# A hybrid attention layer on one core: first loads on two queues, first operations in another order

## What is computed

```python
h = rms_norm(x, norm_pre_g[layer])
proj = jnp.einsum('bsd,de->bse', h, w_in[layer])
q_a, k_a, v_a, g_a, f_a, q_b, k_b, v_b, g_b = jnp.split(proj, offsets, axis=-1)
log_f = jax.nn.log_sigmoid((f_a + fox_forget_b[layer]).astype(jnp.float32))
y_a = fox_attention(..., log_f)     # 8 heads of 64, causal, with F = cumsum(log_f) added to the logits
y_a = merge_heads(y_a) * jax.nn.silu(g_a)
y_b = moba_attention(..., slopes)   # 8 heads of 64, causal with ALiBi (a single block here)
y_b = merge_heads(y_b) * jax.nn.silu(g_b)
y = jnp.einsum('bse,ed->bsd', jnp.concatenate([y_a, y_b], axis=-1), w_out[layer])
x = x + rms_norm(y, norm_post_g[layer])
```

## Time and profile before

| | us |
|---|---|
| median of 3 executions | 163.12 |
| lowest and highest | 162.9 and 168.15 |
| span of the profiled execution | 161.2 |
| DVE busy | 124.8 (77%) |
| ACT busy | 112.3 (70%) |
| POOL busy | 72.0 (45%) |
| bytes moved | 27.99 MB, mean 174 GB/s |

### The profile page before, as it was taken

The page is one execution under the profiler, slowest core; times in us unless marked ns, Lnnn a source line. Parts: engine busy times, 40 slices in busy tenths (PEclk is TensorE's granted clock), DMA queues, the critical chain, the costliest instruction groups (busy, mean ns, idle before and its releaser), DMA issues.

```text
span 161.2 us, 2896 instructions
## 1 busy us (share of the span) xinstructions
PE 146.4 (91%) x976; PEld 129.1 (80%) x976; DVE 124.8 (77%) x257; ACT 112.3 (70%) x228; POOL 72.0 (45%) x74
## 2 busy tenths in 40 slices
PE   7699999999958999999798999999998989999950
PEld 7267678889948999988687999998988867889850
DVE  0479976589999989685998989898989989340583
ACT  3589549398835874989959898979969696305330
POOL 7205910000960999504608475744719083501130
PEclk9999999999999999999999999999999999999998
DMA  3999376646796895591556455552526090000024
GB/s 56 304 413 355 123 247 217 250 130 242 262 372 205 357 296 193 169 256 69 150 179 185 140 172 159 139 189 64 157 108 195 0 319 10 0 0 0 4 85 175
DMA packets 12044, 27.99 MB, mean 174 GB/s; under 512 B 1272, under 2 KB 5376, under 8 KB 11776
## 3 DMA queue, kind: packets, MB, share of 16 engines
q1 hardware_dynamic: 11728, 26.52, 49.5%
q10 hardware_dynamic: 304, 1.32, 2.3%
HBM read 24.68 MB, written 1.06 MB: 160 GB/s over the span
## 4 chain that ended last, share of the span: by engine, by line
PE 33%; issue 25%; DVE 16%; POOL 12%; ACT 7%; DMA 3%; SPq 1%; POOLq 1%; DVEq 0%; ACTq 0%
PE bank L791 11%; PE bank L932 10%; PE bank L775 5%; POOL probs L302 5%; DVE w_lo L538 4%; DVE h L616 4%; POOL bias L285 3%; DMA raw<-in_w_units 3%; POOL bias L294 2%; ACT w_hi L354 2%; PE bank L805 2%; DVE h_lo L622 1%; PE bank L885 1%; POOL xg_lo L308 1%; ACT gate L469 1%
## 5 line engine op out<-in xcount | busy, mean ns | idle before, releaser
L538 DVE TENSOR_TENSOR w_lo<-raw,w_hi 128x1024 fp32r<-128x1024 f32 x35 | 51.4, 1475 | 3.7 <-ACT w_hi L354 3.4
L354 ACT ACTIVATE w_hi<-raw 128x1024 fp32r<-128x1024 f32 x35 | 36.8, 1057 | 6.9 <-PE bank L775 2.1
L775 PE MATMUL bank<-h_hi,w_hi 128*128 128x256 f32 x128 | 35.9, 280 | 0.0
L775 PE MATMUL bank<-h_lo,w_hi 128*128 128x256 f32 x128 | 35.8, 279 | 0.0
L775 PE MATMUL bank<-h_hi,w_lo 128*128 128x256 f32 x128 | 35.7, 279 | 0.0
L302 POOL TENSOR_TENSOR probs<-probs,row_inv 128x256 f32<-128x256 f32 (+1 forms) x16 | 12.9, 829 | 36.4 <-DVE row_inv L654 36.4
L313 POOL TENSOR_TENSOR wo_lo<-raw_out,wo_hi 128x1024 fp32r<-128x1024 f32 x4 | 17.4, 4350 | 24.6 <-ACT wo_hi L358 24.6
L775 PEld LDWEIGHTS bank<-h_hi,w_hi 128*128 128x128 f32 x128 | 24.2, 189 | 0.5 <-DVE h_lo L622 0.2
L775 PEld LDWEIGHTS bank<-h_lo,w_hi 128*128 128x128 f32 x128 | 24.0, 188 | 0.2
L775 PEld LDWEIGHTS bank<-h_hi,w_lo 128*128 128x128 f32 x128 | 24.2, 189 | 0.0
L775 PE MATMUL bank<-xg_hi,w_hi 128*128 128x256 f32 x64 | 17.9, 280 | 2.5 <-DVE gate L612 2.5
(11 more groups left out here) (127 smaller groups left out, 336.7 us busy)
## 6 DMA issues: line engine op xcount, KB each, us to landing
raw<-in_w_units SPq DMA_DIRECT2D x31, 512.0 KB, 4.1
raw_out<-in_w_out SPq DMA_DIRECT2D x4, 512.0 KB, 4.5
v_pair<-v SPq DMA_DIRECT2D x8, 256.0 KB, 4.3
raw<-in_w_out SPq DMA_DIRECT2D x4, 512.0 KB, 3.5
x_t<-in_xt SPq DMA_DIRECT2D x4, 256.0 KB, 5.5
squares<-decay_rows_scratch ACTq DMA_DIRECT2D x1, 1024.0 KB, 7.8
x_t<-in_x SPq DMA_DIRECT2D x1, 1024.0 KB, 5.2
out<-x_t SPq DMA_DIRECT2D x3, 256.0 KB, 2.1
```

The costliest lines, as they stand in the source:

```text
L354: nc.scalar.activation(w[0][:, s, :], raw[:, s, :], ACT.Copy).then_inc(s_hi, 1)
L538: nc.vector.tensor_tensor(w[1][:, s, :], raw[:, s, :], w[0][:, s, :].bitcast(F32), ALU.subtract).then_inc(s_lo, 1)
L775: last = nc.tensor.matmul(dst, stationary(a, j), moving(b, j), start=n == 1, stop=n == count * len(PASSES))
```

## The change

SP no longer issues `gpre`, `wf` and the two halves of unit 0; ACT issues them ahead of everything else, in the order first half, `gpre`, second half, `wf`. On ACT the high part of the first half stands between the first and the second `xg_hi`. On DVE the low half, `wf` and the second half are interleaved with `xg_lo`. On PE `value_half(0, 0)` stands ahead of `forget(0)`, and `value_half(0, 1)` ahead of `forget(1)`. And `value_half` waits ahead of each pass, for the parts that this pass reads.

```diff
-            sp.dma_start(gpre_col[:, :], g_pre).then_inc(s_g_in, 16)
             for c in range(X_LOADS):
                 sp.dma_start(x_t[:, n * c:n * c + n, :], xt[:, n * c:n * c + n, :]).then_inc(s_x_in[c], 16)
-                if c == 0:
-                    sp.dma_start(wf[:, :, :], w_f).then_inc(s_wf_in, 16)
-                    sp.dma_start(raw[:, c, 0:HALF], w_units[c, :, 0:HALF]).then_inc(s_raw_half, 16)
-                if c == 0:
-                    sp.dma_start(raw[:, c, HALF:], w_units[c, :, HALF:]).then_inc(s_raw_in[c], 16)
-                else:
+                if c > 0:
                     sp.dma_start(raw[:, c, :], w_units[c]).then_inc(s_raw_in[c], 16)
...
+            act.dma_start(raw[:, 0, 0:HALF], w_units[0, :, 0:HALF]).then_inc(s_raw_half, 16)
+            act.dma_start(gpre_col[:, :], g_pre).then_inc(s_g_in, 16)
+            act.dma_start(raw[:, 0, HALF:], w_units[0, :, HALF:]).then_inc(s_raw_in[0], 16)
+            act.dma_start(wf[:, :, :], w_f).then_inc(s_wf_in, 16)
             act.wait_ge(s_ones, 1)
...
                     nc.scalar.activation(xg[0][:, j, :], x_t[:, j, :], ACT.Copy,
                                          scale=gpre_col[:, j:j + 1]).then_inc(s_xghi, 1)
+                    if j == 0:
+                        act.wait_ge(s_raw_half, 16)
+                        nc.scalar.activation(w[0][:, 0, 0:HALF], raw[:, 0, 0:HALF], ACT.Copy).then_inc(s_half_hi, 1)
                 if c == 0:
-                    act.wait_ge(s_raw_half, 16)
-                    nc.scalar.activation(w[0][:, 0, 0:HALF], raw[:, 0, 0:HALF], ACT.Copy).then_inc(s_half_hi, 1)
...
+            x_low(0)
+            dve.wait_ge(s_half_hi, 1)
+            nc.vector.tensor_tensor(w[1][:, 0, 0:HALF], raw[:, 0, 0:HALF], w[0][:, 0, 0:HALF].bitcast(F32),
+                                    ALU.subtract).then_inc(s_half_lo, 1)
+            dve.wait_ge(s_wf_in, 16)
+            nc.vector.tensor_tensor(wf[:, :, :], wf[:, :, :],
+                                    gpre_col[:, :].unsqueeze(2).to_broadcast((P, KT, HEADS)), ALU.mult).then_inc(s_wfg, 1)
+            x_low(1)
+            dve.wait_ge(s_hi, 1)
+            nc.vector.tensor_tensor(w[1][:, 0, HALF:], raw[:, 0, HALF:], w[0][:, 0, HALF:].bitcast(F32),
+                                    ALU.subtract).then_inc(s_lo, 1)
...
-                if u == 0 and n == 0:
-                    pe.wait_ge(s_half_lo, 1)
-                else:
-                    pe.wait_ge(s_lo, u + 1)
-                if c == 0:
-                    pe.wait_ge(s_xglo, j + 1)
                 for a, b in PASSES:
+                    if u == 0 and n == 0:
+                        pe.wait_ge((s_half_hi, s_half_lo)[b], 1)
+                    else:
+                        pe.wait_ge((s_hi, s_lo)[b], u + 1)
+                    if c == 0:
+                        pe.wait_ge((s_xghi, s_xglo)[a], j + 1)
                     for t in range(TT):
...
+            value_half(0, 0)
             pe.wait_ge(s_wfg, 1)
             forget(0)
-            value_half(0, 0)
+            value_half(0, 1).then_inc(s_used, 1)
             forget(1)
-            value_half(0, 1).then_inc(s_used, 1)
             value_unit(1)
```

More of the change, by code:

```diff
@@ L541, in _, with x_low @@
             dve.wait_ge(s_g_in, 16)
[L542 to L554, removed]
+            def x_low(j):
                 dve.wait_ge(s_xghi, j + 1)
@@ L558, in _ @@
                                                op1=ALU.subtract).then_inc(s_xglo, 1)
+            x_low(0)
[9 more added lines that the diff above has]
+                                    ALU.subtract).then_inc(s_lo, 1)
+            for c in range(1, X_LOADS):
+                x_low(2 * c)
+                x_low(2 * c + 1)
+                if c < X_LOADS - 1:
+                    unit_low(c, c + 1)
             for u in range(X_LOADS - 1, 7):
```

## The result

| | before | changed |
|---|---|---|
| median, us | 163.33 (4 runs) | 166.26 (4 runs, 165.91 to 166.52) |
| ratio | 1 | 1.0177, interval 1.0143 to 1.021 |
| span of the profiled execution, us | 161.2 | 164.3 |
| start of rrow on DVE, us | 30.05 | 33.24 |

The forecast was 163.8 us with a range of 162.0 to 165.6: the way was right, the size was not. 2.9 us were lost in the medians, 3.1 in the profiled spans, not 0.65. In the last comparison of the experiments the changed kernel came out at 1.0188 (1.0127 to 1.025). In part of the executions of all these kernels the granted clock fell near 50 us, and from rrow to the output product the profiled ones took 105.8 to 106.1 or 107.5 to 107.6 us instead of 103.0, so beside the times I compare where rrow starts, which lies ahead of that.

A forecast was written before the change was run, and what follows sets the result against it. PE's early work was taken to bound the kernel, its delay reaching the end. Start +0.55, shape +0.1, waits 0 and rest 0 gave +0.65 us on 163.12, so 163.8 us, whole range 162.0 to 165.6.

The forecast's parts named there:

- What bounds the kernel: PE's early matmuls: PE is busy from 9.65 to 35.10 us, and delay ahead passes one for one to the end.
- What the change has to beat: PE's start of real work: 6.25 us plus 0.07 idle, 6.32 and not 8.20, since forget(0) ran from 6.25.
- What is A?: Start of xg_hi(0) on ACT: 5.7 us, bounds 5.2 to 6.6; x and half unit landed by 6.33 at the latest.
- As long as before: Half-pace stretch of PE's first matmuls: assumed unchanged in length, shifting with the start, no cost beyond the 0.55 us.
- Rival R2: PE's pace rises later: half pace 3.4 us longer, 1.7 us of work lost on top, 165.5 us; chance 0.15.
- The change of shape: Value products following a forget product once more on a never idle PE: 0.12 us for 18 matmuls, 0.1 added.
- the waits cost nothing: Waits ahead of each pass on PE, 32 new places: cost zero, with 0.6 us kept for the range.
- cover: wf, last on ACT's queue, wanted at about 9.3 us: cover about 1 us, by the second x chunk's landing before 8.10.
- R3: Another DVE-GpSimd stall in h: 2.5 us on PE, up to 4.1, giving 166.3 to 167.9 us; chance 0.06.
- R4: The existing DVE-GpSimd stall in h falls away: 163.8 less 2.5 is 161.3 us; chance 0.04.
- R1: First loads there at 4.4 us, so PE starts at 5.6 and gains 0.7 us: 162.5 us; chance 0.2.
- start of PE's real work: First value matmul on PE at A + 1.18 = 6.88 us, 0.55 later than 6.32; bounds +0.05 and +1.45.

## Why the prediction missed

**What bounds the kernel: right.** PE is never idle from its first value matmul to rrow, and a shift at 30 us arrives whole at the end (102.98 and 103.02 us from rrow to the output product).

**What the change has to beat, 6.32 us and not 8.20: right.** The order on PE alone cost 1.29 us at rrow in one execution each, more than the 0.56 between the two executions of the kernel before. This is the cost that the diff hides: forget(0) looked like work in the way and was work in an empty place.

**The step that failed is "What is A?".** A was set to 5.7 us within 5.2 to 6.6, and came out at 7.79. x and the half unit, at 5.9 and 6.1 us, stayed within the upper bound of 6.33; x alone would have put A at 5.9. The wrong bound was gpre's: I put it 0.3 us behind the half unit, as wf had come behind x. That row was of a single queue. With a second one feeding 512 KB loads beside it, the lag was 1.6 us, and 0.2 us when SP held them back. gpre has 4 KB, but they go to 128 partitions in 128 pieces of 32 bytes. That each of these takes turns with a large piece of the other queue is a reading that fits both lags, but it is not shown: the pieces were not traced one by one, and it does not say why gpre took 2.2 us at the head of one queue and 4.5 at the head of the other. The rule of the Trainium skill on interleaving (DMA: Bandwidth & Descriptors, Issuing engines are not separate DMA queues) pointed the right way, and I had weighed it for the large loads only. The trace agrees for these, with x and the half unit at 5.9 and 6.1 us. The rest of the path was right: from A to the first value matmul passed 1.08 us, where the forecast has 1.18.

**PE's pace: mis-sized.** "As long as before" was 3.4 us; it was 4.1 to 4.6 twice, and about 5.5 once. That is 0.43 us of the loss: 4.62 us for the half unit and forget(0) against 4.19 without the 0.07 of idle time that the 6.32 already counts. Rival R2 had this mechanism at 1.7 us and was partly true, on top of the late start rather than in its place. Why the changed kernel got the longer stretch three times is not settled. PE's idle time of 4.1 us ahead of it suggests itself, but with SP held back PE had idled 2.0 us and stayed at half pace for longer still, to 12.8 us. What is shown is that filling this time removes the half pace.

**The change of shape: mis-sized.** The forecast has 0.1 us, and 0.21 were measured behind forget(0). The single matmuls show where they go: at each switch from value to forget products and back, one spacing is 0.33 or 0.34 us instead of 0.23, and there is one more forget product among the value products at full pace.

**Right:** the waits cost nothing (5.61 us for 24 matmuls); the low half came at 9.54, in time for the second pass at 9.88; the second half and wf were covered, wf narrowly, ready at 11.13 us for a product that started at 11.72. wf landed at 2.14 + 8.7 = 10.8 us, far later than the 8.10 of the second x chunk, from which the forecast took its cover: it held only because PE itself was late, and with the longer warm-up PE waited 0.2 us for wf. The stall between DVE and GpSimd moved along unchanged, so R3 and R4 did not occur, nor did R1.

| term | forecast | measured |
|---|---|---|
| start of PE's real work | +0.55 | +2.55: about 1.3 by the order on PE (6.32 to 7.59), 1.3 by the loads (7.59 to 8.87, of which gpre 1.6, less 0.3 that the other loads gained) |
| half pace | 0 | +0.43 |
| change of shape | +0.1 | +0.21 |
| waits | 0 | 0 |
| sum at rrow | +0.65 | +3.19 |

## What to carry to other kernels

Before work is moved out of the way of the critical path, ask what the engine did with the time ahead: work that runs while nothing else could is free there and costs in any other place. A small load on which everything hangs belongs ahead of the large ones, and its lag is to be taken from a row with the same neighbours on the other queue, not from a quiet one. And a stretch at half pace at the start can be removed with matmuls on ones up to the first real one, but the gain is kept only as far as the loads allow. Such a repair is to be given to the kernel before as well, or it hides what the change itself costs: 0.7 to 1.2 us here.

## What was not expected of the hardware

- 4 KB in 128 pieces landed 1.6 us after their issue at the head of the only queue, 2.2 us at the head of SP's with 256 KB on ACT's, 4.5 us at the head of ACT's with x on SP's, and 6.6 us behind 256 KB on ACT's.
- Loads issued later hold up one issued before: in the changed kernel x chunk 0 took 5.2 us and the half unit 5.4, and 4.5 and 4.7 when SP issued nothing behind the chunk.
- Of two loads of 256 KB on two queues the one ahead can win by far. Issued together they took 5.2 and 5.4 us. With the half unit 0.43 us ahead it took 2.8 us and x chunk 0 5.0; with x chunk 0 0.45 us ahead it took 4.3 and the half unit 5.6.
- PE's pace at the start differs between executions of the same kernel. forget(0) of the kernel before took 1.88 us in one and 1.03 us in another, with the granted clock read as 1.00 over both; in the second the clock then fell to 0.50 from 7.8 to 11.1 us. Ahead of the fall PE had idled for 1.54 us, worked on forget(0) for 1.03 and idled again. 24 matmuls on ones took 4.47, 5.49 and 4.91 us in three executions.
- The granted clock can read 1.00 over matmuls at half pace: 512 columns started 0.43 us apart from 8.87 us on in the changed kernel. In these sixteen executions only falls behind a first rise show in it.
- Near 50 us PE idles 2.5 us for the gate. In some executions the granted clock stayed at 1.00 behind it, in others it fell to 0.50 for 3.3 us (48.2 to 51.5), and the time to the output product grew by 2.9 us.
